# One transformer block in compensated fp32 on one core: the first output-projection pass takes eight chunks instead of six, and its preparation is spread over three attention steps

## The chip, the cores and the metric

The kernel runs on one core of one Trainium2 chip. The metric is device time in microseconds (us) for one launch, the median of three runs.

## The reference, cut to what matters

One block: stick-breaking attention (16 heads), cross-attention into 256 memory tokens (4 heads), one output projection, a gated feed-forward. S = 1024 tokens, D = 1024, all float32.

```python
hn = rms_norm(x, attn_norm)
q, k, v, xq = split_cols(hn @ sb_w_in, [1024, 1024, 1024, 256])
# per head and query t, keys j < t, z = q.k / 8
a[t, j] = exp(log_sigmoid(z[t, j]) + sum_{j < i < t} log_sigmoid(-z[t, i]))
mix = a @ v                                      # 16 heads of 64
cross = cross_attention(xq, mem, ...)            # 4 heads of 64
x = x + concat([mix, cross]) @ w_out             # (1024 x 1280) @ (1280 x 1024)
x = x + (silu(f @ w_gate) * (f @ w_up)) @ w_down # f = rms_norm(x, ffn_norm)
```

## The kernel before, in words

Every product is formed from split operands. A value is copied to a "high" tile (`_h`, done by ACT), the rest is subtracted out into a "low" tile (`_l`, done by DVE or POOL), and TensorE (PE) runs three matmuls: high by high, high by low, low by high. The order of the instructions on each engine is written out by hand, and the engines meet through semaphores only. Each engine works strictly in its own order.

**Attention steps.** The 16 heads form eight pairs, and a *step* s = 0 to 7 handles one pair. Steps 0 to 5 are a hardware loop of three turns with two steps each; step 6 and step 7 (`last=True`) are written out. A step has twelve *units* u = 0 to 11, each a block of 128 queries by up to 512 keys, and one *slot* per unit. For a unit:

- PE forms the scores (L369). ACT takes two sigmoids, `fail` (L455) and `succ` (L461). DVE runs a scan over `fail` for each of the two heads (L555, L560) and multiplies (`dve_weights`, L568): these are the attention weights, in `succ`. After them it copies the last column (L574) where there are more keys to come.
- PE transposes the weights into the banks `t_ps` (L379). It may do that only when the weights are there and when DVE has taken the low part of the unit before out of `t_ps`.
- ACT copies the transposed weights (`a_h`, L469), DVE takes the low part (`a_l`, `dve_low`, L581), and after each odd unit PE multiplies with the values (L395).
- After units 1, 3, 7 and 11, ACT and POOL write 256 query columns of the heads (L480, L481, L588).

Between these, PE in slot u of steps 0 to 6 runs 12 matmuls of the input projection for the next step (L341), and at the end it transposes the next pair's v (L352). ACT and DVE split v (L448, L545). The first transposition of the next step waits for this v, since it is written to the same banks.

**Output projection.** 1280 rows of `w_out` are ten *chunks* k of 128 rows: 0 to 7 belong to the eight head pairs, 8 and 9 to the cross-attention heads. A task i of `pe_project` computes one tile of 128 tokens by 512 columns; one chunk costs three matmuls of 512 columns (L1073). Tasks 0 to 7 are the first pass (left columns, chunks 0 to 5), which lies in the slots of step 7 where the input projection was (`FILL`). Tasks 8 to 15 are the late pass (left columns, chunks 8, 9, 6, 7) behind step 7; DVE adds both (`dve_part`, L1099). Tasks 16 to 23 are the right columns with all ten chunks. Before its use, each half of a chunk's heads (`("o", k, half)`) and each chunk's weights (`("w", k, half)`) must be split: the high part by ACT (L882), the low part (L888) by POOL for the weights of the left columns, by DVE for the rest. Weights come through four buffers `wo_raw`, which SP refills once the low part of the chunk four places before is done. Seven of the early high tiles go to `ex_h` and are moved by DMA later.

## Time and profile before

| | |
|---|---|
| median of 3 runs | 1344.54 us (1344.37 to 1344.92) |
| profiled execution, its own time | 1346.36 us |
| its span in the profile | 1344.6 us |
| PE busy | 1320.3 us (98%) |
| DVE busy | 1033.4 us (77%) |
| ACT busy | 684.7 us (51%) |
| POOL busy | 418.9 us (31%) |

The span reaches from the first to the last instruction; the execution's own time has 1.8 us around it. PE is busy nearly throughout. So a change of order alone can win only what PE stands idle, and it can lose as much as it makes PE wait. Times such as "557.11" in the text are positions in us from the start of the span.

### The profile page before, as it was taken

To read this page: it belongs to the slowest core of one execution; us is meant where nothing else is said; L and a number is where in the kernel's file an instruction comes from. 1 tells how busy PE (TensorE), PEld (TensorE's weight loads), DVE (VectorE), ACT (ScalarE), POOL (GpSimd) and SP (SyncE) were. 2 spreads that over 40 slices of the span, in tenths; PEclk is the share of its full clock that TensorE was granted. 3 is DMA by queue.
4 is the path that set the end of the run, shared out by engine and by line. 5 is a ranking of instruction groups with operands and counts; after the bars stand their busy time and mean duration, and the time that the engine had idled before them with its cause. 6 is when DMAs were issued, how large, how long until landed. Compare 5 with 4: busy or idle time off the path is not lost.

```text
span 1344.6 us, 20557 instructions
## 1 busy us (share of the span) xinstructions
PE 1320.3 (98%) x6854; PEld 1088.3 (81%) x6854; DVE 1033.4 (77%) x1182; ACT 684.7 (51%) x1202; POOL 418.9 (31%) x309
## 2 busy tenths in 40 slices
PE   7999999999999999999999999999999999999999
PEld 4877888888888887778888788888888888888887
DVE  6677889897988989985348877878777787877866
ACT  6667766666676666773245334343333434333340
POOL 1000000000000000313015855647455484654721
PEclk9999999999999999999999999999999999999999
DMA  7100101101000101303301221221212112121103
GB/s 250 32 17 24 39 18 32 32 16 31 23 24 25 37 16 48 102 17 118 102 17 55 63 71 48 63 62 39 63 40 77 55 39 70 31 76 56 48 32 126
DMA packets 91477, 71.76 MB, mean 53 GB/s; under 512 B 4256, under 2 KB 75936, under 8 KB 91424
## 3 DMA queue, kind: packets, MB, share of 16 engines
q1 hardware_dynamic: 91424, 71.07, 17.0%
q8 instruction: 31, 0.51, 0.2%
q14 instruction: 22, 0.18, 0.0%
HBM read 65.03 MB, written 4.19 MB: 51 GB/s over the span
## 4 chain that ended last, share of the span: by engine, by line
PE 89%; DVE 5%; ACT 3%; POOL 1%; issue 1%; DMA 0%; SPq 0%; ACTq 0%; DVEq 0%; POOLq 0%
PE ps L1367 27%; PE ps L341 17%; PE ps L1542 14%; PE ps L1073 7%; PE ps L395 5%; PE ps L379 5%; PE ps L369 4%; PE ps L1152 3%; PE ps L1597 2%; PE ps L310 2%; ACT succ L979 1%; PE ps L849 1%; PE ps L789 1%; DVE succ L568 1%; PE ps L290 1%
## 5 line engine op out<-in xcount | busy, mean ns | idle before, releaser
L1552 DVE TENSOR_TENSOR x<-ps,x 128x2048 f32<-128x2048 f32 x70 | 160.3, 2290 | 92.6 <-PE ps L1542 92.6
L588 POOL TENSOR_TENSOR o_t<-o_t,pv_low 128x256 f32 x24 | 22.6, 944 | 468.9 <-ACT o_t L481 468.9
L1335 DVE TENSOR_TENSOR part_l<-part_x,part_h 128x512 fp32r<-128x512 f32 x140 | 141.7, 1036 | 25.3 <-POOL part_x L1313 17.9
L1530 POOL TENSOR_TENSOR bl<-bx_B,bh 128x512 fp32r<-128x512 f32 x70 | 93.0, 1329 | 208.9 <-ACT bh L1526 208.9
L341 PE MATMUL ps<-hh,w_h 128*128 128x512 f32 x336 | 140.6, 418 | 0.0
L469 ACT ACTIVATE a_h<-ps 128x256 fp32r<-128x256 f32 (+2 forms) x96 | 78.0, 813 | 121.0 <-PE ps L379 120.5
L341 PE MATMUL ps<-hh,w_l 128*128 128x512 f32 x336 | 131.9, 393 | 0.0
L341 PE MATMUL ps<-hl,w_h 128*128 128x512 f32 x336 | 131.4, 391 | 0.0
L1367 PE MATMUL ps<-ft_h,part_h 128*128 128x512 f32 x320 | 124.5, 389 | 0.0
L1367 PE MATMUL ps<-ft_l,part_h 128*128 128x512 f32 x320 | 124.5, 389 | 0.0
L1367 PE MATMUL ps<-ft_h,part_l 128*128 128x512 f32 x320 | 124.5, 389 | 0.0
L581 DVE TENSOR_TENSOR a_l<-ps,a_h 128x256 fp32r<-128x256 f32 (+2 forms) x96 | 91.5, 954 | 38.3 <-ACT a_h L469 37.8
L1378 ACT ACTIVATE kept<-ps 128x512 f32<-128x512 f32 x60 | 35.7, 595 | 158.2 <-PE ps L1367 158.2
L1542 PE MATMUL ps<-bh,ah 128*128 128x512 f32 x280 | 109.1, 390 | 0.9 <-DVE x L1552 0.7
L1542 PE MATMUL ps<-bl,ah 128*128 128x512 f32 x280 | 108.9, 389 | 0.0
L555 DVE TENSOR_TENSOR_SCAN fail<-fail,own 128x129 f32<-128x129 f32 (+3 forms) x128 | 104.8, 846 | 0.0
L1526 ACT ACTIVATE bh<-bx_B 128x512 fp32r<-128x512 f32 x70 | 44.2, 631 | 102.5 <-PE ps L1542 98.0
L568 DVE TENSOR_TENSOR succ<-fail,succ 128x256 f32<-128x256 f32 (+2 forms) x96 | 94.5, 985 | 0.3
L1367 PE MATMUL ps<-f_h,part_h 128*128 128x512 f32 x240 | 93.4, 389 | 0.0
L1367 PE MATMUL ps<-f_l,part_h 128*128 128x512 f32 x240 | 93.4, 389 | 0.0
L1367 PE MATMUL ps<-f_h,part_l 128*128 128x512 f32 x240 | 93.4, 389 | 0.0
L1328 ACT ACTIVATE part_h<-part_x 128x512 fp32r<-128x512 f32 x140 | 82.9, 621 | 19.6 <-POOL part_x L1302 14.7
(286 smaller groups left out, 3395.7 us busy)
## 6 DMA issues: line engine op xcount, KB each, us to landing
w_raw<-in_sb_w_in SPq DMA_DIRECT2D x52, 256.0 KB, 2.8
bx_B<-in_w_down SPq DMA_DIRECT2D x44, 256.0 KB, 3.0
part_x<-in_w_gate SPq DMA_DIRECT2D x40, 256.0 KB, 2.9
part_x<-in_w_up SPq DMA_DIRECT2D x40, 256.0 KB, 2.9
wo_raw<-in_w_out SPq DMA_DIRECT2D x20, 256.0 KB, 2.9
x_in<-in_x SPq DMA_DIRECT2D x8, 512.0 KB, 8.1
x<-in_x SPq DMA_DIRECT2D x16, 256.0 KB, 5.4
out<-x SPq DMA_DIRECT2D x16, 256.0 KB, 2.0
```

Of the source, the lines that this page charges most:

```text
L341: mm = pe.matmul(j_ps[:, 0], w[:, kc // 4, kc % 4], h[:, kc, half * BANK:(half + 1) * BANK], start=(kc == 0 and i == 0), stop=(kc == KC - ...
L469: act.activation(a_h[:, :, 0:w // P, col * P:(col + 1) * P], t_ps[:, :, 0:w].rearrange("p h (j q) -> p h j q", q=P), ACT.Copy).then_inc(s_ ...
L555: dve.tensor_tensor_scan(back, back, own[:, BANK - w:BANK + 1][:, ::-1], 0.0, ALU.mult, ALU.max).then_inc(s_scan, 1)
L568: done = dve.tensor_tensor(g, f[:, :, 1:w + 1], g, ALU.mult)
L581: dve.tensor_tensor(a_l[:, :, 0:w // P, c], t_ps[:, :, 0:w].rearrange("p h (j q) -> p h j q", q=P), a_h[:, :, 0:w // P, c].bitcast(F32), A ...
L1073: mm = pe.matmul(out_bank(i), o[:, t % 4 * P:t % 4 * P + P], w[k][:, :], start=(at_ == 0 and j == 0), stop=(at_ == len(order) - 1 and j == 2))
L1328: act.activation(part_h[p][:, :, :].rearrange(flat), part_x[m][p][:, :, :].rearrange(flat), ACT.Copy).then_inc(s_fh, 1)
L1335: dve.tensor_tensor(part_l[m][p][:, :, :].rearrange(flat), part_x[m][p][:, :, :].rearrange(flat), part_h[p][:, :, :].rearrange(flat).bitca ...
L1367: mm = pe.matmul(product_bank(m, p), w[:, k], g[:, k], start=(p in (0, 1, 3) and k == 0 and i == 0), stop=(k == 3 and i == 2), skip_group_ ...
L1530: pool.tensor_tensor(bl[(par + k) % 2][:, :], bx[B_OPS[k]][:, :], bh[(par + k) % 2][:, :].bitcast(F32), ALU.subtract).then_inc(s_bw, 1)
L1542: mm = pe.matmul(ps[:, t], g[:, t * P:(t + 1) * P], w[:, :], start=(k in (0, 4, 5) and i == 0), stop=(i == 2), skip_group_check=True)
L1552: dve.tensor_tensor(o, ps[:, 0:4], o, ALU.add).then_inc(s_x2, 1)
```

## The change: what it does

- The first pass takes chunks 0 to 5, 8 and 9 (24 matmuls per task, before 18), the late pass chunks 6 and 7 (6 per task, before 12). The number of matmuls stays the same: 8 x 24 + 8 x 6 = 8 x 18 + 8 x 12.
- Steps 4 and 5 leave the hardware loop, so that each can have instructions of its own. The early splits of the heads, seven of them in step 6 before, now lie in steps 4 to 6, in slot 5 and at the end of each step; on DVE the ones of a last slot come in `dve_open`, between the next step's weights and v.
- Three splits (`PRE_END`: heads of chunk 9, weights of chunks 4 and 5) stand on ACT between step 6's heads and the first `fail` of step 7; two of them came later before, one was in slot 8 of step 7.
- In slot 1 of step 7, DVE takes the low part before the scans. One piece of the first task (chunk 0) is run by PE ahead of the first transposition of step 7.
- `FILL` gives the slots of step 7, from 0 to 11, these numbers of matmuls: 9 (three of them ahead of the transposition), 9, 6, 24, 12, 12, 24, 24, 24, 24, 12, 12. Before it was 9, 9, 9, 9, 18, 9, 9, 18, 9, 9, 18, 18.
- The late pass rotates over four banks, before over two. SP fetches all of `w_out` before any of x, and POOL starts its additions (`pool_part`) only when the last weights are split.

```diff
-        EX = [("o", k, 0) for k in range(6)] + [("o", 0, 1)]
+        EX = [("o", k, 0) for k in (8, 0, 1, 2, 3, 4, 5)]
...
                     if u == 0:
+                        pe_project(pe, 0, some=(0,))
                         pe_transposes(pe, s, u)
...
                 act_high(act, s, u)
-                if isinstance(s, int) and s == PAIRS - 2:
-                    for i in PRE_AT.get(u, ()):
+                if isinstance(s, int):
+                    for i in PRE_AT.get((s, u), ()):
                         act_split(act, i)
...
             act_low_rows(act, s, NU - 1)
+            if isinstance(s, int) and s == PAIRS - 2:
+                for i in PRE_END:
+                    act_split(act, i)
...
-        def dve_open(dve, s, par):
+        def dve_open(dve, s, par, between=()):
             dve_scan(dve, s, 1, 0)
             dve_scan(dve, s, 1, 1)
             dve_weights(dve, s, 1)
+            for i in between:
+                split_low(dve, i)
             dve_v(dve, par, TUSE * s)
...
+                if last and u == 0:
+                    split_low(dve, PRE_END[0])
+                if last and u == 1:
+                    dve_low(dve, s, u)
                 if nxt and u:
                     dve_scan(dve, *nxt, 0)
...
-        PRE_AT = {1: [EX[0]], 4: [EX[1]], 5: [EX[2]], 8: [EX[3]], 9: [EX[4]],
-                  10: [("w", 0, 0), ("w", 1, 0), EX[5]], 11: [("w", 2, 0), ("w", 3, 0), EX[6]]}
+        EARLY_ORDER = (0, 1, 2, 3, 4, 5, 8, 9)
+        LATE_ORDER = (6, 7)
+        PEELED = PAIRS - 4
+        PRE_AT = {(PEELED, 5): [EX[0]], (PEELED, NU - 1): [EX[1], EX[2]],
+                  (PEELED + 1, 5): [EX[3]], (PEELED + 1, NU - 1): [EX[4]],
+                  (PEELED + 2, 5): [EX[5]], (PEELED + 2, NU - 2): [("w", 0, 0), ("w", 1, 0)],
+                  (PEELED + 2, NU - 1): [EX[6], ("w", 2, 0), ("w", 3, 0)]}
+        PRE_END = [("o", 9, 0), ("w", 4, 0), ("w", 5, 0)]
...
-        SPLIT_RATE = (2, 1, 1, 1, 1, 1, 1, 1, 2, 2, 2, 0)
-        DVE_RATE = (0, 0, 1, 1, 1, 1, 1, 0, 1, 1, 1, 1)
+        SPLIT_RATE = (2, 1, 1, 2, 1, 1, 2, 0, 1, 1, 2, 1)
+        DVE_RATE = (0, 1, 1, 1, 2, 1, 1, 1, 0, 0, 0, 3)
+        FILL = {0: [(0, (1, 2))], 1: [(0, (3, 4, 5))], 2: [(0, (8, 9))], 3: [(1, None)], 4: [(2, (0, 1, 2, 3))],
+                5: [(2, (4, 5, 8, 9))], 6: [(3, None)], 7: [(4, None)], 8: [(5, None)], 9: [(6, None)],
+                10: [(7, (0, 1, 2, 3))], 11: [(7, (4, 5, 8, 9))]}
...
-            return j_ps[:, i % 2 if i >= ALONE else 0]
+            return ps[:, 2 if i < ALONE else (2, 4, 5, 3)[i % 4] if NT <= i < 2 * NT else 2 + i % 2]
...
         def pool_part(pool, t):
+            if t == 0:
+                wait_split(pool, SECOND[-1])
...
-        LOOPS = (PAIRS - 2) // 2
+        LOOPS = (PAIRS - 4) // 2
```

The order on ACT from the split of v to the first units of step 7, before (`om_t` and `pv_low` are the last heads of step 6, `wo_h` the high parts of chunks' weights):

```order
L448 ACTIVATE v_s_71<-ps 128x8x2x64
L480 ACTIVATE pv_low<-ps 64x256
L481 ACTIVATE om_t<-ps 64x256
L480 ACTIVATE pv_low<-ps 64x256
L481 ACTIVATE om_t<-ps 64x256
L455 ACTIVATE fail<-ps 128x2x384
L469 ACTIVATE a_h<-ps 128x2x128
L882 ACTIVATE wo_h_106<-wo_raw 128x512
L461 ACTIVATE succ<-ps 128x2x384
L882 ACTIVATE wo_h_107<-wo_raw 128x512
L469 ACTIVATE a_h<-ps 128x2x2x128
```

The same place in the changed kernel, from the last head rows (its line numbers are higher by 1 to 30):

```order
L482 ACTIVATE om_t<-ps 64x256
L904 ACTIVATE o_h_141<-o_t 128x512
L904 ACTIVATE wo_h_106<-wo_raw 128x512
L904 ACTIVATE wo_h_107<-wo_raw 128x512
L456 ACTIVATE fail<-ps 128x2x384
L470 ACTIVATE a_h<-ps 128x2x128
L904 ACTIVATE wo_h_110<-wo_raw 128x512
L462 ACTIVATE succ<-ps 128x2x384
L904 ACTIVATE wo_h_111<-wo_raw 128x512
L470 ACTIVATE a_h<-ps 128x2x2x128
```

Three copies now stand ahead of `fail` of unit 2 and of the first `a_h`, none before; five stand ahead of the second `a_h`, two before.

On DVE, from unit 1's weights to unit 3's at the opening of step 7, before:

```order
L568 TENSOR_TENSOR succ<-fail,succ 128x2x256
L545 TENSOR_TENSOR v_s_71<-ps,v_s_71 128x8x128
L581 TENSOR_TENSOR a_l<-ps,a_h 128x2x128
L555 SCALAR_TENSOR_TENSOR fail<-fail,own 128x385 x2
L581 TENSOR_TENSOR a_l<-ps,a_h 128x2x2x128
L568 TENSOR_TENSOR succ<-fail,succ 128x2x384
L555 SCALAR_TENSOR_TENSOR fail<-fail,own 128x513 x2
L581 TENSOR_TENSOR a_l<-ps,a_h 128x2x3x128
L568 TENSOR_TENSOR succ<-fail,succ 128x1024
```

The same in the changed kernel:

```order
L572 TENSOR_TENSOR succ<-fail,succ 128x2x256
L910 TENSOR_TENSOR o_l_153<-o_t,ex_h_171 128x512
L549 TENSOR_TENSOR v_s_71<-ps,v_s_71 128x8x128
L910 TENSOR_TENSOR o_l_161<-o_t,o_h_141 128x512
L585 TENSOR_TENSOR a_l<-ps,a_h 128x2x128
L585 TENSOR_TENSOR a_l<-ps,a_h 128x2x2x128
L559 SCALAR_TENSOR_TENSOR fail<-fail,own 128x385 x2
L572 TENSOR_TENSOR succ<-fail,succ 128x2x384
L910 TENSOR_TENSOR o_l_144<-o_t,o_h_124 128x512
L559 SCALAR_TENSOR_TENSOR fail<-fail,own 128x513 x2
L585 TENSOR_TENSOR a_l<-ps,a_h 128x2x3x128
L572 TENSOR_TENSOR succ<-fail,succ 128x1024
```

The low part of unit 1 (`a_l`, 128x2x2x128) has moved ahead of unit 2's scans, and three splits of heads (`o_l`) have come in; one of them stood ahead of unit 1's scans before.

On PE, the first transpositions of step 7 (L379 `succ`) with the projection between them, in the changed kernel:

```order
L1103 MATMUL ps<-wo_h_102,ex_h_166 128x512
L1103 MATMUL ps<-wo_l_112,ex_h_166 128x512
L1103 MATMUL ps<-wo_h_102,o_l_143 128x512
L379 MATMUL ps<-ident,succ 128x128 x2
L1103 MATMUL ps<-wo_h_103,ex_h_167 128x512
L1103 MATMUL ps<-wo_l_113,ex_h_167 128x512
L1103 MATMUL ps<-wo_h_103,o_l_145 128x512
L1103 MATMUL ps<-wo_h_104,ex_h_168 128x512
L1103 MATMUL ps<-wo_l_114,ex_h_168 128x512
L1103 MATMUL ps<-wo_h_104,o_l_147 128x512
L379 MATMUL ps<-ident,succ 128x128 x4
```

Before, all nine matmuls stood between the two transpositions; now three stand ahead of the first.

## Rows read from the trace of the kernel before

**Rows 1.** Windows: step 6, then step 7. Columns: window, length, busy us per engine.

```profile
493.80:555.90 62.10, 60.91 (x378) 50.20 (x376) 57.81 (x70) 44.89 (x75) 9.23 (x8) 1.00 0.16 49
555.90:618.70 62.80, 58.57 (x346) 47.37 (x345) 51.83 (x56) 42.82 (x70) 12.98 (x10) 1.00 0.16 54
```

**Rows 2.** Waits of PE from 440 to 640: us in total, times, longest.

```profile
PE ps L395 <- DVE a_l L581: 1.2, 2, 0.9
PE ps L379 <- DVE succ L568: 1.2, 3, 0.6
PE ps L379 <- DVE v_s L545: 1.2, 1, 1.2
PE ps L1073 <- POOL wo_l L888: 0.9, 1, 0.9
PE ps L379 <- DVE fail L574: 0.7, 1, 0.7
PE ps L1073 <- DVE part L1099: 0.5, 1, 0.5
PE ps L1073 <- ACT part L1088: 0.3, 1, 0.3
```

**Rows 3.** Timeline of PE, opening of step 7: start, us, instruction, idle before.

```profile
557.11 0.41 PE L379 MATMUL ps<-ident,succ 128*128 128x128 f32 x2 [1.16 <-DVE v_s L545]
...
559.45 0.60 PE L379 MATMUL ps<-ident,succ 128*128 128x128 f32 x4
...
564.35 0.84 PE L379 MATMUL ps<-ident,succ 128*128 128x128 f32 x6
...
568.22 0.98 PE L379 MATMUL ps<-ident,succ 128*128 128x128 f32 x7
```

**Rows 4.** Timeline of ACT, opening of step 7.

```profile
557.23 0.81 ACT L455 ACTIVATE fail<-ps 128x768 f32<-128x768 f32 x1
557.94 0.38 ACT L469 ACTIVATE a_h<-ps 128x256 fp32r<-128x256 f32 x1
558.20 0.64 ACT L882 ACTIVATE wo_h<-wo_raw 128x512 fp32r<-128x512 f32 x1
558.73 0.82 ACT L461 ACTIVATE succ<-ps 128x768 f32<-128x768 f32 x1
```

**Rows 5.** Timeline of DVE, opening of step 7.

```profile
558.35 0.42 DVE L581 TENSOR_TENSOR a_l<-ps,a_h 128x256 fp32r<-128x256 f32 x1 [1.39 <-ACT a_h L469]
558.69 2.86 DVE L555 TENSOR_TENSOR_SCAN fail<-fail,own 128x385 f32<-128x385 f32 x2
562.05 1.38 DVE L568 TENSOR_TENSOR succ<-fail,succ 128x768 f32<-128x768 f32 x1
563.36 2.33 DVE L555 TENSOR_TENSOR_SCAN fail<-fail,own 128x513 f32<-128x513 f32 x2
566.07 0.96 DVE L581 TENSOR_TENSOR a_l<-ps,a_h 128x768 fp32r<-128x768 f32 x1 [0.39 <-ACT a_h L469]
```

**Rows 6.** The same scans and weights in loop step 5, POOL idle.

```profile
436.45 1.80 DVE L555 TENSOR_TENSOR_SCAN fail<-fail,own 128x385 f32<-128x385 f32 x2
438.75 0.95 DVE L568 TENSOR_TENSOR succ<-fail,succ 128x768 f32<-128x768 f32 x1
```

**Rows 7.** Timeline of POOL, opening of step 7.

```profile
558.92 3.70 POOL L888 TENSOR_TENSOR wo_l<-wo_raw,wo_h 128x512 fp32r<-128x512 f32 x2 [0.89 <-ACT wo_h L882]
```

**Rows 8.** Timelines of DVE and PE in the loop: v of step 5, units 10 and 11.

```profile
433.39 1.23 DVE L545 TENSOR_TENSOR v_s<-ps,v_s 128x1024 fp32r<-128x1024 f32 x1 [2.08 <-ACT v_s L448]
...
481.11 0.52 PE L379 MATMUL ps<-ident,succ 128*128 128x128 f32 x3
...
484.49 1.22 DVE L568 TENSOR_TENSOR succ<-fail,succ 128x1024 f32<-128x1024 f32 x1
```

**Rows 9.** Timeline of DVE in the late pass.

```profile
624.08 0.69 DVE L1099 TENSOR_TENSOR part<-ps,part 128x512 f32<-128x512 f32 x1
624.68 0.68 DVE L888 TENSOR_TENSOR wo_l<-wo_raw,wo_h 128x512 fp32r<-128x512 f32 x1
```

More of the change, by code:

```diff
@@ L608, in dve_step @@
                     dve_w(dve, s + 1 + LOW_AT[u] // 6, LOW_AT[u] % 6, (1 - par + LOW_AT[u] // 6) % 2)
-                dve_low(dve, s, u)
+                if not (last and u == 1):
+                    dve_low(dve, s, u)
                 if nxt and u:
                     dve_weights(dve, *nxt)
-                if isinstance(s, int) and s == PAIRS - 2:
-                    for i in PRE_AT.get(u, ()):
-                        if LOW[i][0] == 1:
-                            split_low(dve, i)
+                if u < NU - 1:
+                    for i in early_halves(s, u):
+                        split_low(dve, i)
                 if last:
@@ L873, in act_split @@
             if i in PRE and what == "o":
-                act.wait_ge(s_o, 4 * (k + 1) + 1)
+                if k < PAIRS:
+                    act.wait_ge(s_o, 4 * (k + 1) + 1)
+                else:
+                    act.wait_ge(s_co, CU)
             if what == "o" and k >= PAIRS - 2 and k < PAIRS:
@@ L1054, in pe_project @@
             last = i == 3 * NT - 1
-            order = (range(EARLY), LATE_ORDER, LAST_ORDER if last else range(OC))[i // NT]
+            order = (EARLY_ORDER, LATE_ORDER, LAST_ORDER)[i // NT]
             if i == ALONE:
                 pe.wait_ge(s_fg, 2 * NU * PAIRS)
-            elif 0 < i < NT + 2:
-                pe.wait_ge(s_pt, i - (i > ALONE))
-            elif i:
+            elif i == NT:
+                pe.wait_ge(s_pt, ALONE)
+            elif i == NT + 3:
+                pe.wait_ge(s_pt, NT)
+            elif 0 < i < ALONE:
+                pe.wait_ge(s_pt, i)
+            elif NT + 4 <= i <= 2 * NT:
+                pe.wait_ge(s_x2, i - NT - 3)
+            elif i == 2 * NT + 1:
+                pe.wait_ge(s_x2, NT)
+            elif i > 2 * NT:
                 pe.wait_ge(s_x2, i - NT - 1)
@@ L1776, in _ @@
                         load_w(sp, 2 * m + par + 1, k)
-            for k in range(6):
-                load_w(sp, PAIRS - 1, k)
+            for s in range(PEELED + 1, PAIRS):
+                for k in range(6):
+                    load_w(sp, s, k)
             sp.wait_ge(s_wl, W1)
@@ L1840, in _ @@
                         pool_heads(pool, 2 * m + par, u)
+            for s in range(PEELED, PAIRS - 2):
+                for u in GROUP_END:
+                    pool_heads(pool, s, u)
             for u in GROUP_END:
@@ L1951, in _ @@
                     act_step(act, 2 * m + par, par)
-            act_step(act, PAIRS - 2, 0)
+            for s in range(PEELED, PAIRS - 1):
+                act_step(act, s, s % 2)
             act_step(act, PAIRS - 1, 1, last=True)
@@ L2084, in _ @@
                     dve_step(dve, 2 * m + par, par)
-            dve_step(dve, PAIRS - 2, 0)
+            for s in range(PEELED, PAIRS - 1):
+                dve_step(dve, s, s % 2)
             dve_step(dve, PAIRS - 1, 1, last=True)
@@ L2206, in _ @@
                     pe_step(pe, 2 * m + par, par)
-            pe_step(pe, PAIRS - 2, 0)
+            for s in range(PEELED, PAIRS - 1):
+                pe_step(pe, s, s % 2)
             pe_step(pe, PAIRS - 1, 1, last=True)
```

42 lines of the change are left out of this document (20 added, 22 removed).

## The prediction

> **What bounds the kernel now.** I read the windows by stage first. In step 7, PE is busy 58.57 of 62.80 us, in step 6 60.91 of 62.10 [rows 1]: PE sets the pace, and only there it leaves gaps, 4.2 and 1.2 us. Then the waits of PE from 440 to 640 say who is late [rows 2]: seven kinds, 6.0 us in all, and that is everything a new order can win, since the number of matmuls stays. The three waits for the weights `succ` (1.2 us) lie in step 6, where seven splits of heads had been squeezed between DVE's own work. The rest lies at the opening of step 7 (v: 1.2; chunk weights from POOL: 0.9), later in it (`a_l` 1.2, L574 0.7, the copied part 0.3), and in the late pass (0.5). The timelines of the opening [rows 3 to 5] show the chain that I price: PE transposes unit 0 at 557.11, ACT copies it at 557.94, DVE has its low part at 558.77, PE transposes unit 1 at 559.45. It fits because ACT needs only one `fail` ahead of the copy, and PE has nine matmuls to run meanwhile.
>
> I sum against the profiled execution: 1346.36 us, a span of 1344.6 us with 1.8 us around it. The median of three is 1344.54, 1.8 below it; I carry the difference over. "Now" means the changed kernel at before's positions; what step 6 gains beforehand is booked by itself.
>
> **Steps 4 to 6.** Before, seven splits in step 6 cost PE 1.2 us in three waits [rows 2], 0.4 on average. Now slot 5 of each of the three steps keeps one split, and slot 10 of step 6 keeps POOL's subtractions beside DVE's weights. The splits at a step's end go between weights and v, where DVE idles 2.08 us for ACT [rows 8]; one or two splits of about 0.6 us (the pitch of such a subtraction is 624.68 - 624.08 = 0.6, [rows 9]) are hidden there. If that cover were gone, v would be late and with it the first transposition. I take 0.25 for each of four places (bounds 0 and 0.4): 1.0 against 1.2, a gain of 0.2. ACT has time for its copies in these steps: it is busy 44.89 of 62.10 us even in step 6 [rows 1].
>
> **Opening of step 7, up to unit 3's transposition.** This is the main term.
>
> (a) PE runs chunk 0, three matmuls, before the first transposition. One costs about 0.23 (559.45 - 557.11 = 2.34 for two transpositions, 0.2, and nine matmuls, [rows 3]), so 0.7 of the 1.16 us of waiting for v is filled. Unit 0 is still transposed at about 557.0 or 557.1: v is bound by ACT's copy of v, which does not move.
>
> (b) ACT has three copies ahead of `fail`. A copy takes 558.73 - 558.20 = 0.53, `fail` 557.94 - 557.23 = 0.71 [rows 4]. They begin at 557.23, so `fail` begins at 558.8 and the copy of unit 0 at 559.5, 1.6 later than before. DVE's low part starts 0.41 behind it (558.35 - 557.94) and lasts 0.42: done at 560.3. PE may transpose unit 1 at 560.45. It has only six matmuls for the time from 557.2 and is through at 558.7: a wait of 1.8 (as idle time some 0.15 less). Before there was none here. Ahead of DVE's low part now stands a split that was in slot 8; it fits in DVE's idle 1.39 us [rows 5].
>
> (c) ACT now converts chunk 8's weights, takes `succ` (about 0.7), converts chunk 9's, and copies unit 1 at 559.76 + 0.53 + 0.7 + 0.53 = 561.5. The copy is done at 562.1, the low part at 562.75, and the values of unit 1, after nine matmuls from 560.8, begin at 562.95: almost no wait, so the 0.9 us wait for POOL's chunk weights is gone. Only now come the scans of unit 2, before at 558.69 and now at 562.75, because they stand behind unit 1's low part. With POOL subtracting they take 561.47 - 558.69 = 2.8 [rows 5], without it 1.80 [rows 6]; the weights 1.38 or 0.95. POOL now has five pieces of work here (chunks 4, 5, the heads, 8, 9), at 3.70 / 2 = 1.85 each beside DVE [rows 7]; it is busy until about 565.5. So I take 2.75 for the scans and 0.9 for the weights: done 566.4. Bounds: 1.72 + 0.87 (done 565.35) and 2.8 + 1.38 (done 566.95). Before, unit 2 was transposed at 564.35 [rows 3]. PE is through with the values at 563.9: a wait of 2.4.
>
> (d) Slot 2: DVE has one split more (0.6), the scans of unit 3 (2.3), the low part (0.9) and the weights (about 1.15, the pitch of the full unit's row in [rows 8]) [rows 5], so unit 3 can be transposed at 566.4 + 4.9 = 571.3. PE has six matmuls instead of nine and is through at 569.6: a wait of 1.7. Before it was at 568.22 [rows 3], after 27 matmuls; now 24. The opening so costs 571.3 - 568.2 = 3.1 and the three missing matmuls 0.7: **3.8 lost** (bounds 2.8 and 4.5).
>
> **Rest of step 7.** With 24 matmuls (5.5 us) in most slots, DVE, which needs some 5 us for a full unit (scans 2.3, low part 1.2, weights 1.2, [rows 5, 8]), is ahead. The later waits of before disappear: `a_l` 1.2, L574 0.7, the copied part 0.3, together 2.2. Slot 10 has only 12 matmuls and no scores. In the loop, from unit 10's transposition at 481.11 to unit 11's weights at 485.7 go 4.6 us [rows 8]; PE in slot 10 has about 1.0 for the transpositions (0.98 for seven in [rows 3]) and 2.8 for the matmuls: **0.8 new** (bounds 0.3 and 1.0). Behind it are the 12 matmuls of slot 11, as many as in the loop: nothing.
>
> **Late pass.** Six matmuls are 1.4 us per task; DVE needs 0.69 for the addition and 0.68 for a split [rows 9], pitch 1.2 together. Four banks give it a lead of four tasks, and the 0.5 us wait for `part` goes: 0.5 gained. That x is loaded later and POOL adds later lies behind the last pass, 240 matmuls of 0.23 us, 55 us; nothing in it waits for the right columns of x before task 18. If this cover failed, task 18 would be late.
>
> **Sum.** 3.8 + 0.8 - 2.2 - 0.5 - 0.2 = +1.7 us: 1348.0 us for the profiled execution, 1346.2 us as a median. Its own range, from the bounds: opening 2.8 to 4.5, slot 10 0.3 to 1.0, steps 4 to 6 from 0.0 to 1.6 instead of 1.0; that is -0.8 to +3.2, so 1343.7 to 1347.8 us.
>
> **Rivals.**
>
> A, faster: ACT's three copies do not delay the chain, since ACT was early enough to have them done when PE's transposition ends, and DVE then runs the opening as in a loop step. For it speaks that in the loop PE never waits there with just six matmuls between the transpositions; against it, that ACT's head rows end at 557.2 in before, at the very moment of the transposition [rows 4]. Then of the 6.0 us of [rows 2] only about 0.45 (v), 0.8 (slot 10) and 1.0 (steps 4 to 6) remain: -3.7, 1340.8 us. It decides in favour if unit 1 is transposed by 559 and unit 3 by 567.
>
> B, slower: POOL and DVE hinder one another more than before, over the whole opening. Rows say that two scans grow from 1.80 to 2.86 and that a POOL subtraction takes 1.85 [rows 5 to 7]. If scans, weights and splits up to unit 3 all run at that rate (times 1.5), (c) and (d) grow by about 0.5 + 2.0, and the steps before lose their upper bound of 0.6: +4.8, 1349.3 us. It is decided by whether POOL is still busy when unit 3's scans begin.
>
> The Trainium skill ("SBUF — State Buffer", section "SBUF: two separate sides") calls the pair of ports that DVE and GpSimd share an exclusive lock, which a DVE instruction with two SBUF inputs and a GpSimd instruction hold in turn for their whole length. In this trace neither is held for the whole of the other: two scans and two POOL subtractions lie beside one another in 3.9 us, and each grows by half. By the lock, each scan and the weights of unit 2 would wait for one POOL piece of 1.85 us, and the sum would be some 3 us higher, 1349 us, the place of rival B.
>
> C, nothing changes within what can be told: the waits only move. This is my forecast's own neighbourhood, since gains and losses are of one size.
>
> **How the numbers follow.** A measurement of this kernel tells a difference from none at about 0.2%, 2.7 us: below 1341.9 is faster, above 1347.2 slower. My forecast, with C: 0.60; its range pokes out above 1347.2 by a little, 0.05 of it. Rival A: 0.18, B: 0.22. So faster 0.18, same 0.55, slower 0.27. The range for 8 in 10 goes from A's 1340.8, of which I leave the lower half out, to B's 1349.3: 1341.0 to 1349.5 us. The likeliest case's own range stands above.
>
> **What the profile would show.** (a) PE's first wait for `v_s` 0.4 to 0.5 instead of 1.16. (b) three L904 copies ahead of `fail`, unit 0's `a_h` some 2.4 us behind its transposition and a PE wait of 1.6 to 1.8 on `a_l` ahead of unit 1. (c), (d) two waits of about 2 us each for `succ` ahead of units 2 and 3. Then none until unit 11, 0.8 for `succ` there. A wait for `succ` of 0.2 to 0.4 in slots 6 to 7 of steps 4 to 6. PE's idle time from 373 to the end of the late pass near 7 to 8 us, before 5.9. I am wrong if the opening's waits sum to under 3 us, or if the late or last pass shows a wait of PE for `part`, `x` or weights of over 0.5 us.

## The result, and the profile after

The changed kernel takes 1347.35 us (median of 22 runs, 1345.74 to 1348.80), the kernel before 1344.93 beside it. The ratio is 1.0016, 95% interval 1.0010 to 1.0022. So the change costs between 0.1 and 0.2%, by the medians 2.4 us.

The profiled execution after took 1345.96 us, before 1346.36: the reverse order. The difference lies ahead of the attention, where the kernel before ran 3.4 us (24.67 to 28.08) at a granted clock of 0.50, while the changed kernel's stayed at 1.00 there. Also, the profiled execution after is one of the two quickest of its 22 launches: those two have a mean granted clock of 0.999, 19 others have 0.997 and take 1346.68 to 1347.64 us. So the profile shows less lost clock than the usual launch had. I compare *the way* between two fixed places: from the first projection matmul of step 0 to the first matmul of the feed-forward. Timeline of PE, before (start, us, instruction); the second row opens the v transpositions behind step 6, the third is the last matmul with the values:

```profile
132.15 0.50 PE L341 MATMUL ps<-hh,w_h 128*128 128x512 f32 x1
...
553.49 0.49 PE L352 MATMUL ps<-ident,v_t 128*128 128x128 f32 x3
...
618.58 0.28 PE L395 MATMUL ps<-a_l,v_s 128*128 128x256 f32 x1
...
699.52 0.39 PE L1152 MATMUL ps<-f_h,gw_h 128*128 128x512 f32 x1
```

The same of the changed kernel, with its first four transpositions in step 7:

```profile
129.76 0.50 PE L341 MATMUL ps<-hh,w_h 128*128 128x512 f32 x1
...
550.33 0.71 PE L352 MATMUL ps<-ident,v_t 128*128 128x128 f32 x5
...
554.45 0.41 PE L379 MATMUL ps<-ident,succ 128*128 128x128 f32 x2 [0.77 <-DVE v_s L549]
...
557.46 0.63 PE L379 MATMUL ps<-ident,succ 128*128 128x128 f32 x4 [1.20 <-DVE a_l L585]
...
563.74 0.88 PE L379 MATMUL ps<-ident,succ 128*128 128x128 f32 x6 [2.67 <-DVE succ L572]
...
569.02 1.09 PE L379 MATMUL ps<-ident,succ 128*128 128x128 f32 x8 [0.40 <-DVE succ L572]
...
629.85 0.28 PE L395 MATMUL ps<-a_l,v_s 128*128 128x256 f32 x1
...
699.14 0.39 PE L1184 MATMUL ps<-f_h,gw_h 128*128 128x512 f32 x1
```

The way is 567.37 us before and 569.38 after: +2.01. For the price of a projection matmul I take the run of 231 from 624.82 on in the chain of work that ended last, before: 52.67 / 231 = 0.228 us.

| stretch | before | after | matmuls moved | net | predicted |
|---|---|---|---|---|---|
| step 0 to v of step 7 | 421.34 | 420.57 | 0 | -0.77 | -0.2 |
| to unit 3's transposition | 14.73 | 18.69 | 3 fewer, 0.68 | +4.64 | +3.8 |
| to the last values | 50.36 | 60.83 | 51 more, 11.63 | -1.16 | +0.8 - 2.2 |
| to the feed-forward | 80.94 | 69.29 | 48 fewer, 10.94 | -0.71 | -0.5 |

Windows of step 6 and step 7 of the changed kernel, answering to [rows 1], and its waits of PE from 360 to 640, answering to [rows 2]:

```profile
491.89:552.74 60.85, 60.55 (x379) 50.33 (x377) 55.23 (x64) 42.38 (x70) 10.34 (x8) 1.00 0.15 48
552.74:629.97 77.23, 70.96 (x394) 57.94 (x393) 52.02 (x60) 44.60 (x73) 12.23 (x10) 0.98 0.13 45
```

```profile
PE ps L379 <- DVE succ L572: 4.1, 4, 2.7
PE ps L379 <- DVE a_l L585: 1.2, 1, 1.2
PE ps L379 <- DVE v_s L549: 0.8, 1, 0.8
PE ps L395 <- DVE a_l L585: 0.5, 1, 0.5
```

Seven kinds of waits have become four, and step 6 is nearly free of them (1.19 us not busy before, 0.30 now). But the sum is 6.6 us where it was 6.0, and most of it now lies in the opening of step 7. That is 0.6 more, and the way grew by 2.0. What else changed is the clock. Windows of the opening (third column from the right: granted clock of PE as a share of 2.4 GHz):

```profile
560.90:563.74 2.84, 0.17 (x3) 0.02 (x2) 2.81 (x4) 0.53 (x2) 0.12 (x1) 1.00 0.54 181
563.74:569.02 5.28, 4.88 (x24) 3.66 (x24) 5.28 (x6) 3.87 (x9) 0.73 (x1) 0.68 0.00 0
```

Behind the 2.67 us wait the clock is at its lower level, 1.2 GHz, for 5.28 x (1 - 0.68) / 0.5 = 3.4 us. PE counts as busy there but does half the work, so about 1.7 us of delay hides in busy time. And the timeline of DVE, answering to [rows 5], with v ahead of it:

```profile
549.48 2.36 DVE L559 TENSOR_TENSOR_SCAN fail<-fail,own 128x257 f32<-128x257 f32 x2
551.88 0.69 DVE L572 TENSOR_TENSOR succ<-fail,succ 128x512 f32<-128x512 f32 x1
552.48 0.68 DVE L910 TENSOR_TENSOR o_l<-o_t,ex_h 128x512 fp32r<-128x512 f32 x1
553.09 1.22 DVE L549 TENSOR_TENSOR v_s<-ps,v_s 128x1024 fp32r<-128x1024 f32 x1
...
556.89 0.42 DVE L585 TENSOR_TENSOR a_l<-ps,a_h 128x256 fp32r<-128x256 f32 x1 [1.46 <-ACT a_h L470]
559.11 0.69 DVE L585 TENSOR_TENSOR a_l<-ps,a_h 128x512 fp32r<-128x512 f32 x1 [1.80 <-ACT a_h L470]
559.72 2.97 DVE L559 TENSOR_TENSOR_SCAN fail<-fail,own 128x385 f32<-128x385 f32 x2
562.72 0.96 DVE L572 TENSOR_TENSOR succ<-fail,succ 128x768 f32<-128x768 f32 x1
563.60 0.68 DVE L910 TENSOR_TENSOR o_l<-o_t,o_h 128x512 fp32r<-128x512 f32 x1
564.20 2.33 DVE L559 TENSOR_TENSOR_SCAN fail<-fail,own 128x513 f32<-128x513 f32 x2
566.46 0.93 DVE L585 TENSOR_TENSOR a_l<-ps,a_h 128x768 fp32r<-128x768 f32 x1
567.30 1.66 DVE L572 TENSOR_TENSOR succ<-fail,succ 128x1024 f32<-128x1024 f32 x1
```

Twice DVE stands idle for ACT's `a_h` (1.46 and 1.80), then it works without a gap until unit 3's weights are done at 568.96, and PE waits for it. All of unit 3's lateness is there when unit 2's scans begin: 9.4 us behind the v transposition (559.72 - 550.33), before 5.2 (558.69 - 553.49). From there to the end of unit 3's weights it is 9.2 us, before 9.5.

### The profile page after: what moved, and what is told of

It is laid out like the page before. It is cut to its first block, busy times and chain, and to the rows that moved or that the text cites. A ratio compares the mean times of both kernels' runs of the same rounds, so it can differ in the third digit from the quotient of the medians.

```text
span 1344.2 us, 20231 instructions
## 1 busy us (share of the span) xinstructions
PE 1320.4 (98%) x6854; PEld 1089.0 (81%) x6854; DVE 1031.4 (77%) x1182; ACT 685.3 (51%) x1202; POOL 418.0 (31%) x309
## 4 chain that ended last, share of the span: by engine, by line
PE 88%; DVE 6%; ACT 3%; issue 2%; POOL 1%; DMA 0%; SPq 0%; DVEq 0%; ACTq 0%; POOLq 0%
PE ps L1399 27%; PE ps L341 16%; PE ps L1574 14%; PE ps L1103 7%; PE ps L395 5%; PE ps L379 5%; PE ps L369 4%; PE ps L1184 3%; PE ps L1629 2%; PE ps L310 2%; DVE succ L572 1%; ACT succ L1001 1%; PE ps L868 1%; PE ps L808 1%; DVE x_stat L990 1%
## 5 line engine op out<-in xcount | busy, mean ns | idle before, releaser
L592 POOL TENSOR_TENSOR o_t<-o_t,pv_low 128x256 f32 (+1 forms) x24 | 23.3, 972 | 466.2 <-ACT o_t L482 466.2
L559 DVE TENSOR_TENSOR_SCAN fail<-fail,own 128x129 f32<-128x129 f32 (+3 forms) x128 | 107.5, 867 | 0.0
```

What stands on the lines that cost most here:

```text
L559: dve.tensor_tensor_scan(back, back, own[:, BANK - w:BANK + 1][:, ::-1], 0.0, ALU.mult, ALU.max).then_inc(s_scan, 1)
```

## The experiments

Theory O: the opening is late because of the order on ACT and DVE. Theory Q: DVE and POOL lengthen one another's work. Theory D, formed on the way: the opening of step 7 needs a short chain, and any split that stands in it costs, while eight chunks are good later. All intervals are 95%; the median of before beside the runs was 1344.6 to 1345.0 us.

| kernel | median, us | ratio to before | the way, us | unit 3, us | low clock, us |
|---|---|---|---|---|---|
| before / changed | 1344.9 / 1347.35 | 1.0016 (1.0010 to 1.0022) | 567.37 / 569.38 | 14.73 / 18.69 | 0 / 3.4 |
| e1 copies later | 1347.77 | 1.0024 (1.0015 to 1.0034) | 571.62 | 19.65 | 6.8 |
| e2 scans first | 1347.87 | 1.0020 (1.0011 to 1.0029) | 570.13 | 17.51 | 3.4 |
| e3 both | 1347.62 | 1.0021 (1.0012 to 1.0030) | 569.59 | 18.62 | 0 |
| e4 spread alone | 1343.66 | 0.9991 (0.9982 to 1.0000) | 566.92 | 14.83 | 0 |
| e5 light POOL | 1345.81 | 1.0007 (0.9998 to 1.0016) | 568.32 | 17.53 | 3.4 |
| e8 light DVE | 1346.80 | 1.0014 (1.0005 to 1.0023) | 570.21 | 19.17 | 6.8 |
| e6 more matmuls | 1348.65 | 1.0031 (1.0020 to 1.0043) | 569.67 | 18.69 | 3.4 |
| e12 busy wait | 1347.18 | 1.0018 (1.0008 to 1.0027) | 569.50 | 18.67 | 0 |
| e10 late pass alone | 1344.21 | 0.9998 (0.9989 to 1.0007) | 566.67 | 14.70 | 0 |
| e11 late, two banks | 1348.84 | 1.0030 (1.0017 to 1.0042) | 572.31 | 19.18 | 6.8 |
| e7 combined | 1341.45 | 0.9977 (0.9968 to 0.9986) | 564.96 | 15.69 | 0 |
| e9 combined, w4 early | 1340.97 | 0.9973 (0.9963 to 0.9984) | 564.21 | 15.04 | 0 |

"Unit 3" is its transposition, counted from the v transposition; "low clock" is the time at a granted clock of 0.50 during the opening or right behind it. The way and these two are from one profiled execution each, the median from 6 to 22 launches; by the two, a kernel's distance from before differs by up to 1.5 us.

**e1, ACT's three copies behind the first `a_h`** (and DVE's split of chunk 9's heads behind the first low part).

```diff
                 act_high(act, s, u)
+                if last and u == 0:
+                    for i in PRE_END:
+                        act_split(act, i)
...
-            if isinstance(s, int) and s == PAIRS - 2:
-                for i in PRE_END:
-                    act_split(act, i)
```

> The changed kernel, with the three PRE_END splits behind the first a_h of step 7 on ACT, and DVE's split of chunk 9's heads behind the first low part. Theory O (the opening of step 7 is bound by the order on ACT and DVE): PE's wait of 1.2 us ahead of unit 1's transposition goes, but unit 1's a_h stands behind the same number of copies, so the wait comes back ahead of unit 1's values (about 1.1 us) and unit 2's transposition stays where it was: 0 +- 0.4 us against the changed kernel. Rival P (ACT's copies alone make the loss): 1.2 us or more are won. Rival Q (DVE and POOL hinder each other): no difference, and no new wait for the values.

**e2, the scans of unit 2 ahead of the low part in slot 1**, as in the kernel before.

```diff
-                if last and u == 1:
-                    dve_low(dve, s, u)
...
-                if not (last and u == 1):
-                    dve_low(dve, s, u)
+                dve_low(dve, s, u)
```

> The changed kernel, with DVE's scans of unit 2 ahead of unit 1's low part again, as in the kernel before. Theory O: DVE is idle for 1.8 us ahead of that low part, the scans fill it; unit 2 is transposed 1.6 us and unit 3 about 2 us earlier, so about 1.9 us less than the changed kernel, and PE's granted clock does not fall at 564, since its wait of 2.7 us shrinks to under 0.6. Rival P: 0. Rival Q: the scans only meet POOL's work earlier, at most 0.5 us less, and the wait for unit 2 stays over 2 us.

**e3, both.**

> Both edits together. Theory O: about 3 us less than the changed kernel (unit 2 at 561.1 and unit 3 at 566.0 on the changed kernel's scale), so 0.5 to 1 us below the kernel before. Rival P: as the copies alone, 1.2 us less. Rival Q: at most 0.5 us less.

None of the three gained, neither by the median nor on the way. In e1 the wait for `a_l` ahead of unit 1 is gone, as forecast, but the one ahead of unit 2 is larger (3.62 us). In e3 the waits for `succ` are 0.88 ahead of unit 2 and 2.57 ahead of unit 3.

e2 is different inside: unit 2 is transposed 1.8 us earlier than in the changed kernel, counted from the v transposition (forecast 1.6), and unit 3 1.2 earlier (forecast 2). But a wait of 2.58 us stands ahead of unit 3, and then the clock is at 0.50:

```profile
568.46:571.87 3.41, 3.41 (x12) 3.04 (x13) 1.55 (x4) 1.46 (x3) 0.00 (x0) 0.50 0.00 0
```

From unit 3 to the last values e2 takes 62.45 us, the changed kernel 60.83, e3, with a full clock, 60.82. So the order did win 1.2 us, and the slow stretch behind it took 1.6. Of e2's eleven launches, the only one with a mean clock of 1.0 took 1345.21 us, the seven with 0.997 took 1347.68 to 1348.90.

Why e3 stayed late is in the timeline of DVE, where nothing stands in its way any more, and POOL beside it (each row one instruction):

```profile
558.23 2.06 DVE L559 TENSOR_TENSOR_SCAN fail<-fail,own 128x385 f32<-128x385 f32 x1
560.21 1.96 DVE L559 TENSOR_TENSOR_SCAN fail<-fail,own 128x385 f32<-128x385 f32 x1
562.09 0.66 DVE L585 TENSOR_TENSOR a_l<-ps,a_h 128x512 fp32r<-128x512 f32 x1
562.67 2.08 DVE L572 TENSOR_TENSOR succ<-fail,succ 128x768 f32<-128x768 f32 x1
564.68 1.76 DVE L907 TENSOR_TENSOR o_l<-o_t,o_h 128x512 fp32r<-128x512 f32 x1
```

```profile
558.18 1.29 POOL L907 TENSOR_TENSOR wo_l<-wo_raw,wo_h 128x512 fp32r<-128x512 f32 x1 [5.69 <-ACT wo_h L901]
559.42 1.93 POOL L907 TENSOR_TENSOR wo_l<-wo_raw,wo_h 128x512 fp32r<-128x512 f32 x1
561.31 1.38 POOL L592 TENSOR_TENSOR om_t<-om_t,pv_low 128x256 f32<-128x256 f32 x1
562.66 1.27 POOL L907 TENSOR_TENSOR wo_l<-wo_raw,wo_h 128x512 fp32r<-128x512 f32 x1
563.91 1.98 POOL L907 TENSOR_TENSOR wo_l<-wo_raw,wo_h 128x512 fp32r<-128x512 f32 x1
```

The instructions end in turn, DVE and POOL alternating. POOL's first piece ends at 559.47, the first scan at 560.29; the second piece at 561.35, the second scan at 562.17; the head addition at 562.69, and so on to DVE's split at 566.44. Each ends 0.5 to 1.1 us behind the other engine's, about its own length alone less 0.1 to 0.2, as if it began only when the other was through. Only the first piece of POOL (1.29), its fourth (1.27) and `a_l`, which reads PSUM, keep their own length.

Counted from the v transposition (552.11 in e3), the scans begin at 6.1 us instead of 9.4. But the two take 3.94 us, against 2.97 and, with POOL idle, 1.80 [rows 6]; the weights 2.08 against 0.96, the split 1.76 against 0.68. The weights end at 12.6 instead of 13.4, and the split that follows at 14.3 instead of 14.0. In e1 the scans begin where they did (9.4), but POOL's pieces come later and both scans wait: 3.85 us, and unit 2 is 0.9 later. What the order wins, POOL takes back in e3, and the clock in e2. Theory O alone is refuted.

**e5, POOL's part of it.** POOL's four subtractions of the opening cover one column; PE reads chunk 3's low part for chunks 4, 5, 8 and 9.

```diff
+            if i in (("w", 4, 0), ("w", 5, 0), ("w", 8, 0), ("w", 9, 0)):
+                low, src, high = low[:, 0:1], src[:, 0:1], high[:, 0:1]
```

> The changed kernel, but POOL's subtractions for the weights of chunks 4, 5, 8 and 9 in the opening of step 7 cover one column instead of 512 (PE reads chunk 3's low part in their place: part of the computation is left out). Theory Q (POOL and DVE lengthen one another's work in the opening): unit 2's two scans fall from 2.97 to about 1.8 us, unit 3's likewise, the weights to under 1; the waits of PE for succ ahead of units 2 and 3 (3.1 us) fall to under 1.5, the clock stays full, and the way from the first projection matmul of step 0 to the first feed-forward matmul falls by 1.5 to 2.5 us from 569.4. Theory O (what counts is the order on ACT and DVE alone): waits within 0.5 us of the changed kernel's, the way 569.0 or more.

Timeline of DVE of e5:

```profile
561.19 1.80 DVE L559 TENSOR_TENSOR_SCAN fail<-fail,own 128x385 f32<-128x385 f32 x2
```

The scans are back at 1.80 and the wait ahead of unit 2 falls from 2.67 to 1.51; the way falls by 1.06. So hindrance is worth about 1.1 of the 4.6 us, less than the 1.5 I expected. It is one wait: in the changed kernel the first scan took 2.12 us, until POOL's piece ended at 561.02, and the second 0.93. The rest of the opening is late without it.

**e8, DVE's part.** DVE's splits of slots 0 and 1 (heads of chunk 9, right half of chunk 0) cover one column; PE reads the low part of chunk 8 or 1.

```diff
+            if i in (("o", 9, 0), ("o", 0, 1)):
+                low, src, high = low[:, 0:1], src[:, 0:1], high[:, 0:1]
```

> The changed kernel, but DVE's two subtractions in slots 0 and 1 of step 7 (heads of chunk 9 and the right half of chunk 0) cover one column each (PE reads another chunk's low part: part of the computation is left out). If DVE's sum of work sets unit 3's weights, the slot-1 split's 0.7 us comes off the wait ahead of unit 3 and the one in slot 0, which lies in DVE's idle time, gives nothing: waits of PE 0.4 to 0.8 us less, the way 568.6 to 569.0 us. If POOL sets the pace of everything there, no change.

Unit 3's weights come 0.7 us sooner, 17.92 us behind the v transposition (550.63) instead of 18.63 (they start at 567.33 and take 1.22). A window of e8:

```profile
563.60:570.40 6.80, 6.37 (x27) 5.13 (x28) 5.93 (x9) 3.85 (x9) 1.03 (x1) 0.50 0.00 1
```

DVE was done at 568.55, but PE reached unit 3's transposition only at 569.81, and without a wait: its clock was at the lower level for all of 6.8 us, twice as long as in the changed kernel and behind the same wait of 2.67. The forecast gain was there for DVE, and PE could not take it up. (Part of it is POOL's: its head addition began at 567.15 in the changed kernel, ahead of these weights, which took 1.66 us, and at 568.11 in e8, behind their start.) The profiled way is longer by 0.8; the median of this kernel is 0.5 lower than that of the changed one, within what the intervals leave open.

**e6 and e12, work put into the waits.** e6 repeats chunks 1 and 2 (three matmuls each) in slots 0 and 2; e12 repeats chunks 1 to 3 (nine matmuls) ahead of unit 2's transposition. The first task's sum is a different one. First e6, then e12:

```diff
-        FILL = {0: [(0, (1, 2))], 1: [(0, (3, 4, 5))], 2: [(0, (8, 9))], 3: [(1, None)], 4: [(2, (0, 1, 2, 3))],
+        FILL = {0: [(0, (1, 2)), (0, (1,))], 1: [(0, (3, 4, 5))], 2: [(0, (2,)), (0, (8, 9))], 3: [(1, None)], 4: [(2, (0, 1, 2, 3))],
```

```diff
             for u in range(NU):
+                if last and u == 2:
+                    pe_project(pe, 0, some=(1, 2, 3))
                 if u:
                     pe_transposes(pe, s, u)
```

> The changed kernel with six matmuls more in the opening: chunk 1 is run twice in slot 0 and chunk 2 twice in slots 1 and 2 of the first task, three matmuls each (so the first task's sum is a different one). They are 1.4 us of work. If PE only stands dry there because its slots are short (9, 9, 6 matmuls for DVE's full units), they lie wholly in its waits: the wait for succ ahead of unit 2 falls from 2.67 to about 2.0, the one ahead of unit 3 goes, and the total stays within 0.3 us of the changed kernel's (569.4 us on the way); if the clock then stays full, it even gets 0.5 to 0.8 us shorter. If instead PE's own work sets the end there, the time grows by 1.4 us.

> The changed kernel with nine matmuls more (chunks 1 to 3 of the first task once again, so that task's sum is a different one) placed by PE between the values of unit 1 and the transposition of unit 2, where it stands idle for 2.67 us. They are 2.1 us of work. If the fall of PE's granted clock to half in the changed kernel follows from the time without work, the clock stays full in the opening, the nine matmuls lie in the wait (left: 0.5 to 0.6), and PE waits 1.5 us or so for succ ahead of unit 3 instead of 0.4; the way from step 0 to the feed-forward stays at 569.1 to 569.5 us, and the median comes out at or a little under the changed kernel's 1347.4. If the clock falls all the same, the matmuls cost at the half level, and the time grows by 1 to 2 us. If PE's own work set the end here, it grows by 2.1 us.

Timeline of PE of e12, transpositions of units 2 and 3, and the window between them:

```profile
563.91 0.87 PE L379 MATMUL ps<-ident,succ 128*128 128x128 f32 x6 [0.52 <-DVE succ L574]
...
569.19 1.09 PE L379 MATMUL ps<-ident,succ 128*128 128x128 f32 x8 [1.94 <-DVE succ L574]
```

```profile
564.00:569.20 5.20, 3.26 (x25) 2.37 (x25) 5.20 (x6) 3.99 (x9) 0.72 (x1) 1.00 0.00 0
```

Nine matmuls, 2.1 us of work, cost 0.1 us on the way, and the clock stayed full. The wait ahead of unit 3, 1.94 instead of 0.40, is the one I had forecast as 1.7 for the changed kernel: there half of it had turned into slow matmuls. So in this profile the fall of the clock cost nothing of its own. It lay where DVE was late anyway, and DVE's chain sets the opening.

That does not hold for a longer fall. e11 (below) has the changed kernel's opening unchanged, and its profile has 6.8 us at 0.50 behind the same wait of 2.67:

```profile
563.42:570.25 6.83, 6.46 (x28) 5.22 (x29) 6.38 (x9) 3.94 (x9) 1.31 (x1) 0.50 0.01 2
```

Unit 3 is then 0.5 us later (19.18 for 18.69) and the stretch to the last values 0.3 longer (61.11 for 60.83). The launches say the same: the mean clock of 0.997 of the changed kernel's usual launch is, as an estimate, 7 to 9 us at 0.50 in 1345 us. Of e12's ten launches, the five with a mean clock of 1.0 took 1346.07 to 1346.61 us, the other five 1347.74 to 1348.88. The first five stand 1.7 us above the launches of before beside them that have a full clock, too (medians 1346.22 and 1344.49). So the chain is worth about 1.7 to 2.0 us, and the rest of the 2.4 by the medians is probably the clock's. Where the launches without a profile lost it is not shown.

e6 is 0.3 us longer on the way, but 0.2 of it lies ahead of step 7, and unit 3 is where it was (18.69). Its three matmuls in slot 0 filled 0.7 us of the wait for `a_l`; the long wait stayed (2.54), the clock fell too, and the three in slot 2 ran at the lower level. By the median it is 1.3 longer; its seven launches have mean clocks of 0.996 to 0.998.

**e4, the spread alone.** The kernel before, with steps 4 and 5 written out and the seven head splits at the changed kernel's places (slot 5 and the end of steps 4 to 6).

```diff
+        PRE_AT = {(PEELED, 5): [EX[0]], (PEELED, NU - 1): [EX[1], EX[6]],
+                  (PEELED + 1, 5): [EX[2]], (PEELED + 1, NU - 1): [EX[3]],
+                  (PEELED + 2, 5): [EX[4]], (PEELED + 2, NU - 2): [("w", 0, 0), ("w", 1, 0)],
+                  (PEELED + 2, NU - 1): [EX[5], ("w", 2, 0), ("w", 3, 0)]}
```

> The kernel before with one part of the change: steps 4 and 5 out of the loop and the seven early splits of heads spread over the slots 5 and ends of steps 4 to 6; first pass, late pass, loads and step 7 as before. Theory O: this part is a gain of 0.7 to 0.8 us against the kernel before (PE's waits for succ in step 6 fall from 1.2 to 0.3 us), and step 7 opens as before. Rival R (straight-line code in place of two loop steps costs by itself, outside the waits): 0 or slower by up to 1 us although the waits shrink.

Half of the forecast: -0.45 on the way, -1.3 by the median, the interval ending at no change. The three waits for `succ` shrank to 0.2 us, but the wait for v grew:

```profile
PE ps L379 <- DVE v_s L545: 1.7, 1, 1.7
```

The timeline of DVE of the changed kernel above says why: v is split at 553.09 right behind a split of heads, although ACT has its copy of v at 552.43:

```profile
551.40 1.03 ACT L449 ACTIVATE v_s<-ps 128x1024 fp32r<-128x1024 f32 x1 [1.51 <-PE ps L352]
```

The idle time that hides such a split in the loop [rows 8] isn't there at the end of step 6, where POOL's subtractions stretch the two scans to 2.36. It was not there in the kernel before either. There DVE went from the weights to v without a gap, while ACT's copy had ended at 555.60 (554.57 + 1.03):

```profile
555.13 0.69 DVE L568 TENSOR_TENSOR succ<-fail,succ 128x512 f32<-128x512 f32 x1
555.74 1.22 DVE L545 TENSOR_TENSOR v_s<-ps,v_s 128x1024 fp32r<-128x1024 f32 x1
```

**e10, the late pass alone** (kernel before with four banks, `w_out` fetched ahead of x, POOL's additions last), and **e11, the changed kernel with two banks**.

```diff
-            return j_ps[:, i % 2 if i >= ALONE else 0]
+            return ps[:, 2 if i < ALONE else (2, 4, 5, 3)[i % 4] if NT <= i < 2 * NT else 2 + i % 2]
```

> The kernel before with only the late-pass edits: four banks, w_out fetched wholly before x, POOL's additions behind the last split. Its late tasks still have twelve matmuls. If banks are what PE waits for there, the wait for the copied part (0.5 us) goes and the stretch from the last values to the feed-forward falls from 80.94 to 80.2 to 80.5 us, nothing else moves: 1344.5 us. Rival: the wait is for ACT's copy of task 7 or for the splits of the right weights, which banks don't help, and x coming later costs something: 80.9 or more.

> The changed kernel with the late pass on two banks as before. Its tasks have six matmuls, 1.4 us, and DVE needs about 1.25 us for a task's addition and a split, behind which the bank comes free. If four banks are needed, PE waits 0.2 to 0.6 us in most of six tasks: the stretch from the last values to the feed-forward grows from 69.29 to 70.5 to 72. If DVE's pitch is just enough, it grows by less than 0.5.

In e10 the stretch from the last values to the feed-forward is 80.14, before 80.94; no wait of PE is left in it. In e11 it is 71.28, after 69.29, with two waits:

```profile
PE ps L1099 <- ACT part L1114: 0.9, 1, 0.9
PE ps L1099 <- DVE part L1127: 0.5, 1, 0.5
```

Both go the way of the forecast. With tasks of twelve matmuls the three edits of e10 together gain 0.8 (0.5 of it was a wait); with six the banks alone gain 2.0 (1.4 of it waits). So without them the smaller tasks would have lost time; the remaining 0.3 and 0.6 no row shows. Loading x later cost nothing that shows. The rest of e11's 2.9 us on the way is the longer fall of the clock (0.8) and 0.2 ahead of step 7.

**e7, combined.** Spread, four banks and eight chunks for tasks 1 to 7, but the opening as before: no `PRE_END`, scans first, 9 matmuls in each of slots 0 to 2, the first task with six chunks (its chunks 8 and 9 in the late pass).

```diff
-        PRE_END = [("o", 9, 0), ("w", 4, 0), ("w", 5, 0)]
+        PRE_END = []
...
-        SPLIT_RATE = (2, 1, 1, 2, 1, 1, 2, 0, 1, 1, 2, 1)
-        DVE_RATE = (0, 1, 1, 1, 2, 1, 1, 1, 0, 0, 0, 3)
-        FILL = {0: [(0, (1, 2))], 1: [(0, (3, 4, 5))], 2: [(0, (8, 9))], 3: [(1, None)], 4: [(2, (0, 1, 2, 3))],
+        SPLIT_RATE = (2, 1, 2, 2, 2, 2, 2, 0, 1, 1, 2, 1)
+        DVE_RATE = (0, 0, 1, 1, 2, 2, 2, 1, 0, 0, 0, 3)
+        FILL = {0: [(0, (0, 1, 2))], 1: [(0, (3, 4, 5))], 2: [(1, (0, 1, 2))], 3: [(1, (3, 4, 5, 8, 9))], 4: [(2, (0, 1, 2, 3))],
```

> A version of both: splits spread over steps 4 to 6 (as in the kernel before with only that), the opening of step 7 in the old order with 9, 9 and 9 matmuls and six chunks in the first task, tasks 1 to 7 with eight chunks, the late pass over four banks (its first task with four chunks). By theory D (the opening needs the short chain of before, the later slots gain from 24 matmuls a task): -0.5 for steps 4 to 6, about 0 for the opening, -1.1 for the later waits, -0.7 for the late pass: 1342.6 us by median where before is 1344.95, and the way from step 0 to the feed-forward 565.1 us. By the rival (eight chunks cost wherever they begin, since POOL's and DVE's splits for chunks 8 and 9 still lie in slots 1 to 3): 566.5 or more, no better than the spread alone.

**e9, e7 with chunk 4's weights copied between the split of v and the last heads of step 6**, and chunk 0 run by PE ahead of the first transposition.

```diff
-        PRE_END = []
+        PRE_END = [("w", 4, 0)]
...
-            act_low_rows(act, s, NU - 1)
             if isinstance(s, int) and s == PAIRS - 2:
                 for i in PRE_END:
                     act_split(act, i)
+            act_low_rows(act, s, NU - 1)
...
                     if u == 0:
+                        pe_project(pe, 0, some=(0,))
                         pe_transposes(pe, s, u)
```

> The combined version (e7) with two more edits at the opening of step 7: ACT copies chunk 4's weights between the split of v and the last heads of step 6 (POOL, which stands idle 3.4 us there, subtracts them before unit 0 is transposed), and PE runs chunk 0 ahead of the first transposition. Theory D (a copy or a subtraction costs only where it stands ahead of the work that is late): the waits for v (1.67) and for chunk 4's weights (0.85) fall to about 1.0 and 0; DVE's weights for unit 2 then come late by some 0.3 to 0.7, since only one POOL subtraction is left beside its scans. The way from step 0 to the feed-forward 564.96 becomes 563.9 to 564.4 us, the median 1340.8. Theory Q (DVE's and POOL's sum sets the opening anyway): 564.8 or more, the gain turns into waits for succ ahead of units 2 and 3. If the copy ahead of fail hurts as the three of the changed kernel did, a wait for a_l of over 0.5 us stands ahead of unit 1.

Both came out as theory D has it: 564.96 (forecast 565.1) and 564.21 (forecast 563.9 to 564.4) on the way, 3.4 and 3.6 us under the kernel before by the medians beside them. By the median e7 gained 1.2 us more than forecast (1341.45 for 1342.6), e9 what was forecast (1340.97 for 1340.8). The terms inside fit less well: in e7 the opening lost 0.96 us where about 0 was forecast, and the later slots gained 2.1 for 1.1; in e9 a wait of 0.66 for POOL's chunk weights stayed (forecast 0). In neither profile did the clock fall at the opening. Waits of PE in e9, 360 to 720:

```profile
PE ps L379 <- DVE succ L572: 1.7, 3, 0.8
PE ps L379 <- DVE v_s L549: 0.8, 1, 0.8
PE ps L1102 <- POOL wo_l L905: 0.7, 1, 0.7
```

In e7 the opening up to unit 3 is 15.69 us for 27 matmuls (before 14.73), the later slots are 2.1 us better than before, the late pass 0.7 and the steps before 0.5: 0.96 - 2.1 - 0.7 - 0.5 = -2.4. Whether e9 beats e7 is not settled by the launches (0.9963 to 0.9984 against 0.9968 to 0.9986); on the way it is 0.75 shorter.

## Why the prediction came out

Forecast 1346.2 us, +1.7; measured +2.0 on the way and +2.4 by the medians. Place and kind were right: the loss lies in the opening, and the later slots and the late pass give part of it back. That the sum came so near is in part luck. The opening was 0.8 us worse than forecast and the rest of step 7 0.2 worse, the steps before and the late pass were 0.8 better, and the errors nearly cancel. For the profiled execution the sum gave 1348.0 us, measured 1345.96: it started from an execution of before that had lost clock ahead of the attention, and the one after had not. The sum has no term for the clock at all, though in the usual launch it is probably part of the 2.4.

- **Steps 4 to 6**: forecast 0.2 gained, measured 0.77, and 0.5 to 0.7 in the other profiles with these steps. I took 0.25 us for each of four places; slot 10 of step 6 costs 0.23, and the three slots 5 cost 0.05 to 0.07 each. In a slot of 12 matmuls DVE has room for one split.
- **(a)**: "unit 0 is still transposed at about 557.0 or 557.1: v is bound by ACT's copy of v" is a step that failed. It was transposed 0.5 us later, 4.12 behind the v transposition instead of 3.62. v is bound by DVE here, and so it was before (rows under e4): the cover taken from [rows 8], a loop turn, is absent at the end of step 6. The wait is 0.77, not 0.45.
- **(b)**: three copies ahead of `fail`, a wait of 1.20 for `a_l` ahead of unit 1, forecast 1.6 to 1.8. With (a) it gives unit 1 at 7.13 instead of 5.96: 1.2 late, forecast 1.0.
- **(c)**: a wait of 2.67 ahead of unit 2, forecast 2.4. The scans took 2.97 and the weights 0.96 for the 2.75 and 0.9 assumed. The reason was another one: POOL's pieces took 1.3 us each and not 1.85, and were through at 561.02, so only the first scan waited for one. That the scans stand behind the low part costs 1.2 of the 4.0 us by which unit 3 is late (e2), leaving aside the fall of the clock behind it.
- **(d)**: the position is DVE's, as forecast; with (a) and a longer weights row (1.66, beside POOL's head addition) unit 3 comes 4.0 us later, forecast 3.1. The wait in front of it is 0.40 and not 1.7, since the clock had fallen. My account had no such row.
- **Rest of step 7**: 1.2 gained, forecast 1.4. Unit 11's wait is 0.76 (forecast 0.8). L574, the copied part and 0.9 of `a_l` are gone, 0.5 for `a_l` remained at 586.
- **Late pass**: 0.7 gained, forecast 0.5, and e11 shows that the banks carry it.
- **The signs**: PE's waits at the opening sum to 5.0 us (wrong if under 3), and the late pass has none, as forecast. Waits of 0.2 to 0.4 in slots 6 to 7 of steps 4 to 6 did not appear.

Rival A is out: ACT's copies delayed unit 1. But taking them away (e1) did not help, so my (b) was a true delay and not the cause of the end. Rival B is out by its own sign, since POOL was done with its splits at 561.02 and unit 3's scans began at 564.20; e5 gives 1.1 us for the hindrance, of which my sum already held a part.

The exclusive lock of the Trainium skill ("SBUF — State Buffer", section "SBUF: two separate sides") lets an instruction of DVE with two SBUF inputs and one of POOL pass only in turn. My prediction read the trace of before as against it, from merged rows: "each grows by half". Taken one by one, the trace agrees. In e3 scans, weights and split each end 0.5 to 0.8 us behind a POOL piece, and POOL's delayed pieces 0.5 to 1.1 us behind a DVE instruction. What was wrong was the price of "one POOL piece of 1.85 us" for each scan and the weights: only the first scan of the changed kernel met a piece, for 1.2 us.

Open: e5, without the hindrance, still waits 1.51 and 0.78 there. The late start of unit 2's scans (9.4 us behind the v transposition; 6.9 in e2, 6.1 in e3) explains most, but was not split further between ACT's two late `a_h` and DVE's order. No kernel had e3's order with a light POOL, which would price the order alone. To put the last split of step 6 behind v was not tried.
